# Attention of the first block: stationary values, moving turned probabilities, two heads on the two column halves of TensorE, output turned

## The chip, the cores and the metric

The kernel runs on one core of a Trainium2 chip. The metric is the device time of one execution in microseconds (us). Before the change three runs gave 3089.05, 3087.79 and 3084.29 us, median 3087.79 us.

## The reference

The program is two two-layer transformer blocks, one behind the other, on 256 tokens of width 1024, all in fp32. The first block works on two streams, X (the tokens) and Z (256 context tokens). Its token mixing has four branches of 256 columns each: a Fourier mix, neighborhood attention (`na`), a gated linear attention (`gla`) and grouped attention (`gqa`). The two attentions are what the change touches:

```python
s = jnp.einsum('bqhgd,bkhd->bhgqk', q_blk, k).astype(jnp.float32)
p = jax.nn.softmax(s, axis=-1).astype(v.dtype)
return jnp.einsum('bhgqk,bkhd->bqhgd', p, v)
...
out_x = jnp.concatenate([a_x, b_x, c_x, d_x], axis=-1)
...
x = x + mx[5] * (mix_x @ w_out[l])
```

Heads are 64 wide. Four heads and two blocks of 128 queries make 8 units per attention. The mixed result (256 x 1024) is then multiplied by `w_out`. In layer 0 both streams are mixed, in layer 1 only X.

## The kernel before

The work is an ordered list of weight pieces of 1 MB. SP loads each into a ring of four buffers (`wr`). ACT writes the high part of a piece to `wh` (L267), DVE the rest to `wl` (L278), each in two halves, and PE multiplies three times (L120, L121, L122: high by high, low by high, high by low). ACT splits piece m+2 and DVE piece m+1 while PE has piece m. Pieces of the modulation are used whole: PE multiplies them in four column tiles of 32 (L777), and DVE turns or adds the sums (L809, L817, L802).

The small work (norms, attention, turning) is cut into steps and woven in between. Every engine runs through the same pieces and in each piece through the same number of steps (`Piece.steps`, 4, or 1 or 2 for modulation), so a step with a given number lies in the same piece on every engine, but not at the same place in it: PE spreads its steps over a piece's matmuls, DVE does the first half of the next `wl` ahead of its first step, the second half ahead of its second, and a projection's `gated` (L905) or `gated_lo` (L856) ahead of its last two. Each engine's queue is in order.

Attention takes the units in pairs (two heads), 8 pairs per stream and layer: Z in layer 0 with 256 keys, X in layer 0 and X in layer 1 with 512. For a pair: PE's scores (`score`, L1948), DVE's row maximum (`peak`, L1992, or L1989 with the bias of `na`), ACT's exponential with its row sum (`exp`, L1973), PE's transposes of the probabilities (`turn`, L1955), ACT's copy of them to SBUF (`move`, L1979), PE's product with the values (`weigh`, L1963), and DVE's reciprocal of the sums (`invert`, L1997) and scaling of the output into `mix` (`keep`, L2002). In layer 0 (`PairAttention`) a pair takes 6 steps of each engine: score and peak 0 in step 0, peak 1 in step 1, exp 0 and 1 in steps 1 and 2, turn in step 3, move and invert in step 4, weigh and keep in step 5. In layer 1 (`WideAttention`) pairs overlap, a step holding score i, weigh i-2 and turn i-1, beside modulation pieces of one step each. Every fp32 matmul is two records in the trace, a transpose one.

`weigh` has the turned probabilities as the stationary operand (128 columns) and the values as the moving one (64 columns): 2 heads x 4 key blocks x 2 records = 16 for a pair with 512 keys, 8 with 256. `MixTurn` then transposes all of `mix` (16 transposes in two PSUM banks, L2122), ACT and DVE split it into `xt_hi` and `xt_lo` (L2135, L2143), and the projection by `w_out` (`ResidualOut`, four pieces) follows.

Of the kernel before, what the change touches and what calls it, by code (L numbers as in the profile page):

```python
# [196 lines left out]
class Woven:  # L197
# [36 lines left out]
    def queue(self, pieces):  # L234

        for p in pieces:
            p.m, p.u0, p.parted_before = len(self.pieces), self.units, sum(q.parted for q in self.pieces)
            self.units += p.n_units
            self.pieces.append(p)

    def load(self, sp, m):

        if m >= len(self.pieces):
            self.follow.load(sp, m - len(self.pieces))
            return
        if m >= RING:
            sp.wait_ge(self.used.sem, m - RING + 1 + self.pieces[m].held_back)
        src = self.pieces[m].src
        a, b = src.shape[1], src.shape[2]
        dst = self.raw[m % RING][:, 0:a * b].rearrange("p (a b) -> p a b", b=b)  # L250
        sp.dma_start(dst, src).then_inc(self.loaded[m % RING].sem, 16)

# [4 lines left out]
    def hi(self, act, m, h, own=False):  # L257

        if m >= len(self.pieces):
            self.follow.hi(act, m - len(self.pieces), h)  # L260
            return
        if not self.pieces[m].parted or (self.pieces[m] in self.own_hi and not own):
            return
        s, r = m % RING, self.half(m, h)
        if h == 0:
            act.wait_ge(self.loaded[s].sem, self.loaded[s].at(m // RING + 1))
        act.activation(self.high[s][:, r], self.raw[s][:, r], ACT.Copy).then_inc(self.highs.sem, 1)  # L267
# [34 lines left out]
    def whole(self, pe, m):  # L302

        s = m % RING
        pe.wait_ge(self.loaded[s].sem, self.loaded[s].at(m // RING + 1))
        return self.raw[s][:, :].rearrange("p (k n) -> p k n", n=D)
# [38 lines left out]
class Piece:  # L345
# [3 lines left out]

    n_units, steps, fetch, parted, cover, held_back = 1, 4, (), True, 0, 0  # L350

# [3 lines left out]
    def after(self, *stages):  # L355
        self.requires += stages
        return self

    def sp(self, sp):
# [1552 lines left out]
class PairAttention(Stage):  # L1912


    def __init__(self, w, pairs, buf, before, mask=None):
# [13 lines left out]
    def wait_done(self, eng):  # L1929
        eng.wait_ge(self.done.sem, self.done.at(2 * self.n))  # L1930

# [61 lines left out]

    def invert(self, dve, i):
        buf, both = self.buf, slice(2 * (i % 2), 2 * (i % 2) + 2)
        dve.wait_ge(self.probs.sem, self.probs.at(2 * i + 2))
        self.w.dve_link(dve.reciprocal(buf["inv"][:, both, 0:1], buf["sums"][:, both, 0:1]))  # L1997

    def keep(self, dve, i, bank):
        for t in range(2):  # L2000
            dve.wait_ge(self.sums.sem, self.sums.at(2 * i + t + 1))
            dve.tensor_scalar(self.pairs[i][t]["out"], self.w.ps[:, bank + t, 0:HD], self.buf["inv"][:, 2 * (i % 2) + t, 0:1], None,  # L2002
                              ALU.mult).then_inc(self.done.sem, 1)

    def pe(self, pe):
        w = self.w
        self.before(pe)
        for i in range(self.n):
# [6 lines left out]
            self.weigh(pe, i, 4)  # L2015
            for t in range(2):
                w.hold(4 + t, lambda pe_, c=2 * i + t + 1: pe_.wait_ge(self.done.sem, self.done.at(c)))
            yield
# [24 lines left out]


class WideAttention(PairAttention):
# [9 lines left out]
    def pe(self, pe):  # L2055
# [5 lines left out]
        for i in range(n + 2):  # L2061
# [6 lines left out]
            if i >= 2:  # L2068
                if i >= 3:
                    pe.wait_ge(self.done.sem, self.done.at(2 * (i - 2)))  # L2070
                self.weigh(pe, i - 2, 4)
            if 1 <= i <= n:
# [25 lines left out]


class MixTurn(Stage):  # L2100

    n_steps = 4

    def __init__(self, w, mix, pair, need, room):
        super().__init__(w)
        self.mix, self.pair, self.need, self.room = mix, pair, need, room
        self.turned, self.highs, self.moved = w.share("mix_turned", 4), w.share("mix_high", 4), w.share("mix_low", 4)

# [3 lines left out]
    def pe(self, pe):  # L2114
        w = self.w
        for b in range(4):
            self.need(pe, b)
            w.open(pe, 4 + b % 2)
            for i in range(2):
                for t in range(2):  # L2120
                    k = 2 * b + i
                    last = pe.transpose(w.ps[:, 4 + b % 2, i * 256 + t * P:i * 256 + (t + 1) * P], self.mix[:, t, k * P:(k + 1) * P], w.eye)  # L2122
            last.then_inc(self.turned.sem, 1)
            w.hold(4 + b % 2, lambda pe_, n=b + 1: pe_.wait_ge(self.moved.sem, self.moved.at(n)))
            yield

    def view(self, b):
        return self.w.ps[:, 4 + b % 2, :].rearrange("p (k n) -> p k n", k=2)

    def act(self, act):  # L2130
        for b in range(4):
            if b == 0:
                self.room(act)
            act.wait_ge(self.turned.sem, self.turned.at(b + 1))
            act.activation(self.pair[0][:, 2 * b:2 * b + 2, :], self.view(b), ACT.Copy).then_inc(self.highs.sem, 1)  # L2135
            yield

    def dve(self, dve):
        for b in range(4):
            if b == 0:  # L2140
                self.room(dve)
            dve.wait_ge(self.highs.sem, self.highs.at(b + 1))
            dve.tensor_tensor(self.pair[1][:, 2 * b:2 * b + 2, :], self.view(b), self.pair[0][:, 2 * b:2 * b + 2, :].bitcast(F32),  # L2143
                              ALU.subtract).then_inc(self.moved.sem, 1)
            yield

class SecondWoven:
# [4 lines left out]
    def __init__(self, c, base, first):  # L2152
# [13 lines left out]
        self.parts = 0  # L2166
        self.dve_step, self.act_step, self.pool_step = (self.share(f"{e}_link", 0) for e in ("dve", "act", "pool"))

# [1052 lines left out]
def second_block(c, A, x, eye, angles, out, base, first):  # L3221
# [325 lines left out]
    def scalar(act):  # L3547
        w.act_link = Chain(act, w.act_step)
        for s in segments:
            s.run("act", act)  # L3550

    def vector(dve):
        w.dve_link = Chain(dve, w.dve_step)
        for s in segments:
            s.run("dve", dve)

    def gpsimd(pool):
        w.pool_link = Chain(pool, w.pool_step)
        for p_ in pools:
# [143 lines left out]
def first_block(w, A, c):  # L3703
# [102 lines left out]
    class Mixers:  # L3806
# [96 lines left out]
        def attention(self, *ready):  # L3903
            s, z = self.s, self.s is Z

            def near(hh, qt):
                r, n = slice(64 * (hh % 2), 64 * (hh % 2) + 64), slice(64 * hh, 64 * hh + 64)
                keys, vs = zna_k[r, hh // 2, :] if z else self.na_keys[r, hh // 2, :], [zna_v[:, j, n] for j in range(2)]
                u = dict(q=self.na_t[r, hh // 2, qt * P:(qt + 1) * P], keys=keys, v=vs, out=mix[:, qt, 256 + 64 * hh:320 + 64 * hh])
                if not z:  # L3910
# [4 lines left out]
            def grouped(hh, qt):  # L3915
                kv = hh // 2
                n = slice(HD * kv, HD * kv + HD)
                u = dict(q=self.g_t[n, hh % 2, qt * P:(qt + 1) * P], keys=zg_k[n, :] if z else self.gqa_keys[n, :], v=[zg_v[:, j, n] for j in range(2)],
                         out=mix[:, qt, 768 + HD * hh:768 + HD * hh + HD])
                if not z:  # L3920
# [18 lines left out]
            self.turn = MixTurn(w, mix, s.pair, waits(self.na.wait_done, self.gqa.wait_done, self.gla_norm.wait_done, self.fourier.wait_done),  # L3939
                                lambda eng: None)  # L3940
            return both + [self.turn]
# [298 lines left out]
```

## Time and profile before

| what | value |
|---|---|
| median of three runs | 3087.79 us (3084.29 to 3089.05) |
| the profiled execution, its own time | 3091.58 us |
| its span | 3089.8 us |
| mean granted TensorE clock | 0.991 |
| PE, matmul | 2984.7 us busy, 97% |
| PEld, weight load | 2736.9 us, 89% |
| DVE | 1754.1 us, 57% |
| ACT | 1461.9 us, 47% |
| attention of Z, layer 0 | about 430 to 513 us |
| attention of X, layer 0 | about 780 to 890 us |
| attention of X, layer 1 | 1746 to 1793 us |

How to read it: a matmul's duration is longer than the distance to the next one, since matmuls are pipelined, so the cost of a run of matmuls is read from the starts. The profiled execution is 3.8 us above the median of the three runs. The page's line of the chain that ended last is 85% PE.

### The profile page before, as it was taken

The numbers are of one execution on the slowest core, as the hardware profiler recorded it, in microseconds if no ns is written. First come the engines' busy times: TensorE is split into PE (matmuls) and PEld (weight loads), VectorE is DVE, ScalarE is ACT, GpSimd is POOL, SyncE is SP. The second block draws the span as 40 slices with busy tenths as digits, with TensorE's granted clock in tenths as the row PEclk, the third lists the DMA queues.
The fourth block names the chain that finished last, engine by engine and source line by source line (L and its number), as shares of the span: only waits on it lengthen the run. The fifth ranks groups of instructions, "written<-read, shape, count | busy, mean of one in ns | idle before, by whom it ended". The sixth has DMA issues, their size and how long they took to land.

```text
span 3089.8 us, 53353 instructions
## 1 busy us (share of the span) xinstructions
PE 2984.7 (97%) x22944; PEld 2736.9 (89%) x22944; DVE 1754.1 (57%) x2618; ACT 1461.9 (47%) x2162; POOL 152.3 (5%) x148
## 2 busy tenths in 40 slices
PE   8999999999999999999999999999999999999998
PEld 6899888898789998899898889999999989999997
DVE  4446555656447545455655455564766656475655
ACT  4335445453545443444444444455654445565443
POOL 0000000001000000000200000001110101110000
PEclk9999999999999999999999999999999999999999
DMA  7875446664465566765365446554455655445563
GB/s 281 282 237 171 153 156 201 223 197 147 154 202 173 185 199 204 263 226 172 117 197 177 159 156 191 198 172 129 121 175 185 197 190 161 127 130 160 177 197 131
DMA packets 411990, 561.95 MB, mean 182 GB/s; under 512 B 26300, under 2 KB 359020, under 8 KB 411372
## 3 DMA queue, kind: packets, MB, share of 16 engines
q1 hardware_dynamic: 411756, 558.55, 55.7%
q8 instruction: 182, 2.98, 0.4%
q14 instruction: 52, 0.43, 0.0%
HBM read 557.41 MB, written 1.10 MB: 181 GB/s over the span
## 4 chain that ended last, share of the span: by engine, by line
PE 85%; DVE 7%; ACT 3%; DMA 2%; issue 2%; SPq 0%; POOL 0%; DVEq 0%; ACTq 0%
PE psum L120 24%; PE psum L122 24%; PE psum L121 24%; DMA wr<-in_ffn_w_dram 2%; PE psum L777 1%; DVE wl L278 1%; PE psum L2471 1%; PE psum L1238 1%; PE psum L1963 1%; PE psum L2387 1%; PE psum L2462 1%; DVE wl L2221 1%; PE psum L1586 1%; PE psum L128 1%; PE psum L1573 1%
## 5 line engine op out<-in xcount | busy, mean ns | idle before, releaser
L278 DVE TENSOR_TENSOR wl<-wr,wh 128x1024 fp32r<-128x1024 f32 (+1 forms) x558 | 658.8, 1215 | 238.1 <-ACT wh L267 236.6
L267 ACT ACTIVATE wh<-wr 128x1024 fp32r<-128x1024 f32 (+1 forms) x558 | 554.9, 1039 | 247.2 <-DMA wr<-in_ffn_w_dram 224.8
L120 PE MATMUL psum<-xt_hi,wh 128*128 128x256 f32 (+1 forms) x2000 | 565.6, 283 | 4.3 <-DVE wl L278 3.2
L122 PE MATMUL psum<-xt_hi,wl 128*128 128x256 f32 (+1 forms) x2000 | 558.0, 279 | 0.0
L121 PE MATMUL psum<-xt_lo,wh 128*128 128x256 f32 (+1 forms) x2000 | 558.0, 279 | 0.0
L2221 DVE TENSOR_TENSOR wl<-wr,wh 128x1024 fp32r<-128x1024 f32 (+3 forms) x336 | 390.9, 1199 | 124.2 <-ACT wh L2213 123.4
L120 PEld LDWEIGHTS psum<-xt_hi,wh 128*128 128x128 f32 (+1 forms) x2000 | 377.4, 189 | 15.8 <-issue 8.6
L121 PEld LDWEIGHTS psum<-xt_lo,wh 128*128 128x128 f32 (+1 forms) x2000 | 376.9, 188 | 2.3
L122 PEld LDWEIGHTS psum<-xt_hi,wl 128*128 128x128 f32 (+1 forms) x2000 | 377.8, 189 | 0.1
L2213 ACT ACTIVATE wh<-wr 128x1024 fp32r<-128x1024 f32 (+3 forms) x336 | 323.4, 999 | 106.3 <-DMA wr<-in_mlp_w_dram 76.4
L120 PE MATMUL psum<-wh,xt_hi 128*128 128x256 f32 (+1 forms) x1280 | 364.8, 285 | 2.4 <-ACT vv L3378 1.8
L121 PE MATMUL psum<-wl,xt_hi 128*128 128x256 f32 (+1 forms) x1280 | 356.3, 278 | 0.0
L122 PE MATMUL psum<-wh,xt_lo 128*128 128x256 f32 (+1 forms) x1280 | 356.2, 278 | 0.0
L120 PE MATMUL psum<-zt_hi,wh 128*128 128x256 f32 (+1 forms) x1072 | 309.2, 288 | 4.8 <-DVE wl L278 4.1
L121 PE MATMUL psum<-zt_lo,wh 128*128 128x256 f32 (+1 forms) x1072 | 299.6, 279 | 0.0
L122 PE MATMUL psum<-zt_hi,wl 128*128 128x256 f32 (+1 forms) x1072 | 299.4, 279 | 0.0
L120 PE MATMUL psum<-wh,gated_hi 128*128 128x512 f32 x616 | 251.1, 408 | 3.9 <-DVE wl L278 2.7
L120 PEld LDWEIGHTS psum<-wh,xt_hi 128*128 128x128 f32 x1280 | 241.5, 189 | 3.5 <-DVE wl L2221 2.4
L122 PE MATMUL psum<-wh,gated_lo 128*128 128x512 f32 x616 | 243.9, 396 | 0.0
L121 PE MATMUL psum<-wl,gated_hi 128*128 128x512 f32 x616 | 243.5, 395 | 0.0
L122 PEld LDWEIGHTS psum<-wh,xt_lo 128*128 128x128 f32 x1280 | 241.5, 189 | 0.0
L121 PEld LDWEIGHTS psum<-wl,xt_hi 128*128 128x128 f32 x1280 | 241.0, 188 | 0.1
(462 smaller groups left out, 5254.0 us busy)
## 6 DMA issues: line engine op xcount, KB each, us to landing
wr<-in_ffn_w_dram SPq DMA_DIRECT2D x231, 1024.0 KB, 5.4
wr<-in_w_in_dram SPq DMA_DIRECT2D x88, 1024.0 KB, 5.3
wr<-in_w_mod_dram SPq DMA_DIRECT2D x72, 1024.0 KB, 5.1
wr<-in_mlp_w_dram SPq DMA_DIRECT2D x64, 1024.0 KB, 5.4
wr<-in_w_out_dram SPq DMA_DIRECT2D x20, 1024.0 KB, 5.3
wr<-in_mem_w_kv_dram SPq DMA_DIRECT2D x8, 1024.0 KB, 5.1
wr<-in_w_branch_dram SPq DMA_DIRECT2D x16, 512.0 KB, 3.5
wr<-in_w_branch_dram SPq DMA_DIRECT2D x8, 1024.0 KB, 5.2
```

The source lines that it names most:

```text
L120: pe.matmul(out, a[0], b[0], start=first, stop=False)
L121: pe.matmul(out, a[0], b[1], start=False, stop=False)
L122: return pe.matmul(out, a[1], b[0], start=False, stop=last)
L128: pe.matmul(out, eye, eye, start=True, stop=True)
L267: act.activation(self.high[s][:, r], self.raw[s][:, r], ACT.Copy).then_inc(self.highs.sem, 1)
L278: dve.tensor_tensor(self.low[s][:, r], self.raw[s][:, r], self.high[s][:, r].bitcast(F32), ALU.subtract).then_inc(self.lows.sem, 1)
L777: last = pe.matmul(self.group_rows(j), b["silu"][:, at:at + MOD_COLS], cols[:, j], start=(k == 0), stop=(k == 1), tile_position=(0, j * MO ...
L1238: return pe.matmul(out, self.x[:, t, k * P:(k + 1) * P], self.b["diag"][:, t, :], start=True, stop=True)
L1573: last = pe.matmul(w.ps[:, 4, at:at + P], a[:, t, d * P:(d + 1) * P], dec[:, tab, :], start=True, stop=True)
L1586: last = pe.matmul(w.ps[:, 4 + i, pair * 256 + t * P:pair * 256 + (t + 1) * P], src[:, 256 + jt * P:256 + (jt + 1) * P], src[:, it * P:(it ...
L2213: act.activation(self.high[s][:, r], self.raw[s][:, r], ACT.Copy).then_inc(self.highs.sem, 1)
L2221: dve.tensor_tensor(self.low[s][:, r], self.raw[s][:, r], self.high[s][:, r].bitcast(F32), ALU.subtract).then_inc(self.lows.sem, 1)
```

## The change

- `weigh` makes the values the stationary operand (64 columns) and the turned probabilities the moving one (128 columns). The two heads of a pair go to columns 0 to 63 and 64 to 127 of the array and to the two halves of the partitions of one PSUM bank, alternating by key block. The number of matmuls stays. The result is the output turned: features on partitions, queries along the row.
- The row sums now lie along the wrong axis, so the probabilities are scaled before they are turned: `scale` (a reciprocal of one column, then a multiplication of 128 x 256 or 128 x 512 in place) for each head, and `turn` waits for it in place of `exp`. In layer 0 it stands in DVE's steps 2 and 3, in layer 1 ahead of the peaks of the next pair. `invert` is gone, and `keep` is one copy of 128 x 128 in place of two scalings of 128 x 64.
- In layer 1 weigh alternates between banks 4 and 5.
- `mix` holds the two attentions turned, so `MixTurn` transposes only the Fourier and gla parts (8 transposes), and ACT and DVE split the rest from SBUF. Its order is Fourier, gla, na, gqa, each with a wait of its own.
- `OutPiece` loads a piece of the first block's `w_out` with three transfers in place of one, since the rows that belong to gqa come in another order.
- The second block goes on with the link semaphores of the first.

```diff
 class OutPiece(ProjectionPiece):
+    n_loads = 3
...
+        out = [(dst[:, 0:6, :], self.src[:, 0:6, :])]
+        for a in range(2):
+            rows = w2d[6 * P + a * P:6 * P + (a + 1) * P, c0:c0 + cw].rearrange("(b d) n -> d b n", d=HD)
+            out.append((dst[a * HD:(a + 1) * HD, 6:8, :], rows))
...
     def turn(self, pe, i, bank):
         for t in range(2):
-            pe.wait_ge(self.probs.sem, self.probs.at(2 * i + t + 1))
+            pe.wait_ge(self.scaled.sem, self.scaled.at(2 * i + t + 1))
...
     def weigh(self, pe, i, bank):
         m = self.width(i) // P
-        for t in range(2):
-            pe.wait_ge(self.moved.sem, self.moved.at(2 * i + t + 1))
-            for j in range(m):
-                last = pe.matmul(self.w.ps[:, bank + t, 0:HD], self.buf["pt"][:, t, j * P:(j + 1) * P], self.pairs[i][t]["v"][j],
-                                 start=(j == 0), stop=(j == m - 1))
-            last.then_inc(self.sums.sem, 1)
+        pe.wait_ge(self.moved.sem, self.moved.at(2 * i + 2))
+        for j in range(m):
+            for t in range(2):
+                last = pe.matmul(self.w.ps[t * HD:(t + 1) * HD, bank, 0:P], self.pairs[i][t]["v"][j], self.buf["pt"][:, t, j * P:(j + 1) * P],
+                                 start=(j == 0), stop=(j == m - 1), tile_position=(0, t * HD))
+        last.then_inc(self.sums.sem, 1)
...
-    def invert(self, dve, i):
...
+    def scale(self, dve, i, t):
+        buf, n = self.buf, 2 * (i % 2) + t
+        dve.wait_ge(self.probs.sem, self.probs.at(2 * i + t + 1))
+        self.w.dve_link(dve.reciprocal(buf["inv"][:, n, 0:1], buf["sums"][:, n, 0:1]))
+        p = self.probs_of(i, t)[:, 0:self.width(i)]
+        dve.tensor_scalar(p, p, buf["inv"][:, n, 0:1], None, ALU.mult).then_inc(self.scaled.sem, 1)
 
     def keep(self, dve, i, bank):
...
+        dve.wait_ge(self.sums.sem, self.sums.at(i + 1))
+        dve.tensor_copy(self.pairs[i][0]["out"], self.w.ps[:, bank, 0:P]).then_inc(self.done.sem, 1)
...
             self.peak(dve, i, 1, 4)
-            yield from [None] * 3
-            self.invert(dve, i)
             yield
+            self.scale(dve, i, 0)
+            yield
+            self.scale(dve, i, 1)
+            yield from [None] * 2
             self.keep(dve, i, 4)
             yield
...
+            if 1 <= i <= self.n:
+                self.scale(dve, i - 1, 0)
+                self.scale(dve, i - 1, 1)
             if i < self.n:
                 self.peak(dve, i, 0, 0)
                 self.peak(dve, i, 1, 0)
             if i >= 2:
-                self.keep(dve, i - 2, 4)
-            if 1 <= i <= self.n:
-                self.invert(dve, i - 1)
+                self.keep(dve, i - 2, 4 + i % 2)
```

On DVE, pair 1 of Z in layer 0 (counted from 0), at 444 to 451 us of the trace before: L1992 is peak 0 and peak 1, L278 the two halves of a `wl`. Before:

```order
L1992 TENSOR_REDUCE head_neg<-psum 128x1
L809 STREAM_TRANSPOSE mod_turned<-psum 128x256
L817 SCALAR_TENSOR_TENSOR mod<-mod_turned,mod 128x16
L278 TENSOR_TENSOR wl_53<-wr_49,wh_57 128x1024
L1992 TENSOR_REDUCE head_neg<-psum 128x1
L278 TENSOR_TENSOR wl_53<-wr_49,wh_57 128x1024
L856 TENSOR_TENSOR gated_lo<-gated,gated_hi 128x512
L1997 RECIPROCAL head_inv<-head_sums 128x2
L2002 TENSOR_SCALAR mix<-psum,head_inv 128x64 x2
```

The same place in the changed program:

```order
L814 STREAM_TRANSPOSE mod_turned<-psum 128x256
L822 SCALAR_TENSOR_TENSOR mod<-mod_turned,mod 128x16
L280 TENSOR_TENSOR wl_53<-wr_49,wh_57 128x1024
L2013 TENSOR_REDUCE head_neg<-psum 128x1
L280 TENSOR_TENSOR wl_53<-wr_49,wh_57 128x1024
L2018 RECIPROCAL head_inv<-head_sums 128x1
L2020 TENSOR_SCALAR probs_130<-probs_130,head_inv 128x256
L861 TENSOR_TENSOR gated_lo<-gated,gated_hi 128x512
L2018 RECIPROCAL head_inv<-head_sums 128x1
L2020 TENSOR_SCALAR probs_130<-probs_130,head_inv 128x256
L2024 COPY mix<-psum 128x128
```

The first scale (L2018, L2020) stands behind both halves of `wl`, the second also behind `gated_lo`, and PE's transposes of this pair wait for them.

On DVE, one step of X's attention in layer 1, at 1762.7 to 1766.1 us of the trace before. Before:

```order
L809 STREAM_TRANSPOSE mod_turned<-psum 128x256
L817 SCALAR_TENSOR_TENSOR mod<-mod_turned,mod 128x16
L1992 TENSOR_REDUCE head_neg<-psum 128x1 x2
L2002 TENSOR_SCALAR mix<-psum,head_inv 128x64 x2
L1997 RECIPROCAL head_inv<-head_sums 128x2
```

The same step in the changed program:

```order
L814 STREAM_TRANSPOSE mod_turned<-psum 128x256
L822 SCALAR_TENSOR_TENSOR mod<-mod_turned,mod 128x16
L2018 RECIPROCAL head_inv<-head_sums 128x1
L2020 TENSOR_SCALAR probs_180<-probs_180,head_inv 128x512
L2018 RECIPROCAL head_inv<-head_sums 128x1
L2020 TENSOR_SCALAR probs_180<-probs_180,head_inv 128x512
L2013 TENSOR_REDUCE head_neg<-psum 128x1 x2
L2024 COPY mix<-psum 128x128
```

The two scales of the pair before stand ahead of this pair's peaks.

## Rows read from the trace of the kernel before

**Rows 1.** The page, busy time and share of the span of each engine
```profile
PE 2984.7 (97%) x22944; PEld 2736.9 (89%) x22944; DVE 1754.1 (57%) x2618; ACT 1461.9 (47%) x2162; POOL 152.3 (5%) x148
```

**Rows 2.** Waits of PE in 430:900: total us, times, longest
```profile
PE psum L1955 <- ACT probs L1973: 6.5, 5, 2.5
PE psum L120 <- DVE wl L278: 3.8, 3, 1.9
```

**Rows 3.** Timeline of one step in layer 1, PE and PEld: start, us
```profile
1757.68 1.13 PE L1948 MATMUL psum<-na_keys,na_t 64*128 64x512 f32 x4
1758.73 0.52 PEld L1963 LDWEIGHTS psum<-hx,probs_t 128*128 128x128 f32 x4 [0.76 <-issue]
1759.17 0.53 PEld L1963 LDWEIGHTS psum<-z_na_v,probs_t 128*128 128x128 f32 x4
...
1760.46 0.92 PEld L1955 LDWEIGHTS psum<-eye,probs 128*128 128x128 f32 x8
1761.54 1.07 PE L777 MATMUL psum<-wr,silu_cond 128*32 128x256 f32 x16
1761.54 0.59 PEld L777 LDWEIGHTS psum<-wr,silu_cond 128*32 128x32 f32 x16 [0.17 <-issue]
1762.54 0.30 PEld L128 LDWEIGHTS psum<-eye 128*128 128x128 f32 x2 [0.41 <-issue]
```

**Rows 4.** Groups on DVE that price the scale: us busy, mean ns of one
```profile
L1266 DVE TENSOR_SCALAR diag<-eye,row_small 128x128 f32<-128x128 f32 x22 | 5.3, 283 | 0.4
L1997 DVE RECIPROCAL head_inv<-head_sums 128x2 f32<-128x2 f32 x24 | 3.8, 158 | 2.4 <-ACT probs L1973 2.4
L2961 DVE TENSOR_SCALAR x<-x,ln_mv,ln_rstd 128x1024 f32<-128x1024 f32 x3 | 2.4, 809 | 0.0
```

**Rows 5.** Timeline, Z in layer 0: pair 1, then pair 3
```profile
446.43 1.22 DVE L278 TENSOR_TENSOR wl<-wr,wh 128x1024 fp32r<-128x1024 f32 x1
447.16 0.20 PEld L1955 LDWEIGHTS psum<-eye,probs 128*128 128x128 f32 x2 [0.15 <-ACT probs L1973]
447.66 0.69 DVE L856 TENSOR_TENSOR gated_lo<-gated,gated_hi 128x512 fp32r<-128x512 f32 x1
...
466.36 0.60 PE L1955 MATMUL psum<-eye,probs 128*128 128x128 f32 x4
466.56 0.69 DVE L905 TENSOR_TENSOR gated<-silu,psum 128x512 f32<-128x512 f32 x1 [3.39 <-PE psum L122]
```

**Rows 6.** Timeline, X in layer 0, pair 6
```profile
871.16 1.23 DVE L278 TENSOR_TENSOR wl<-wr,wh 128x1024 fp32r<-128x1024 f32 x1 [0.80 <-ACT wh L267]
871.89 0.66 PE L1955 MATMUL psum<-eye,probs 128*128 128x128 f32 x4 [1.00 <-ACT probs L1973]
```

**Rows 7.** Timeline in layer 1: the step of rows 3, then the one with wl
```profile
1757.93 0.17 DVE L817 SCALAR_TENSOR_TENSOR mod<-mod_turned,mod 128x16 f32<-128x16 f32 x1
1758.85 0.69 DVE L1989 CUSTOM_DVE_ANT_1 masked<-psum,na_table 128x512 f32<-128x512 f32 x1 [0.74 <-PE psum L1948]
...
1773.54 1.13 PE L1948 MATMUL psum<-gqa_keys,gqa_t 64*128 64x512 f32 x4
1773.85 2.36 DVE L278 TENSOR_TENSOR wl<-wr,wh 128x1024 fp32r<-128x1024 f32 x2
1776.13 1.28 DVE L1992 TENSOR_REDUCE head_neg<-psum 128x1 f32<-128x512 f32 x2
```

**Rows 8.** Timeline of PE at the end of layer 1's attention, first and last
```profile
1786.32 0.63 PE L1963 MATMUL psum<-hx,probs_t 128*128 128x64 f32 x4
...
1793.58 0.36 PE L120 MATMUL psum<-wh,xt_hi 128*128 128x256 f32 x1 [0.57 <-issue]
```

**Rows 9.** A wait of PE, and windows: busy, then PEclk, DMA share
```profile
789.54 1.11 PE L1955 MATMUL psum<-eye,probs 128*128 128x128 f32 x4 [2.47 <-ACT probs L1973]
...
786.00:797.00 11.00, 8.03 (x46) 7.43 (x44) 2.87 (x5) 5.82 (x9) 0.00 (x0) 0.69 0.40 161
430.00:520.00 90.00, 87.43 (x662) 74.62 (x661) 44.99 (x81) 48.78 (x90) 0.00 (x0) 0.98 0.54 182
```

**Rows 10.** The page's DMA issues, us to landing
```profile
wr<-in_w_out_dram SPq DMA_DIRECT2D x20, 1024.0 KB, 5.3
```

More of the change, by code:

```diff
@@ L250, in load @@
         dst = self.raw[m % RING][:, 0:a * b].rearrange("p (a b) -> p a b", b=b)
-        sp.dma_start(dst, src).then_inc(self.loaded[m % RING].sem, 16)
+        for to, rows in self.pieces[m].transfers(dst):
+            sp.dma_start(to, rows).then_inc(self.loaded[m % RING].sem, 16)
     def half(self, m, h):
@@ L265, in hi @@
         if h == 0:
-            act.wait_ge(self.loaded[s].sem, self.loaded[s].at(m // RING + 1))
+            act.wait_ge(self.loaded[s].sem, self.loaded[s].at(self.pieces[m].landed))
         act.activation(self.high[s][:, r], self.raw[s][:, r], ACT.Copy).then_inc(self.highs.sem, 1)
@@ L304, in whole @@
         s = m % RING
-        pe.wait_ge(self.loaded[s].sem, self.loaded[s].at(m // RING + 1))
+        pe.wait_ge(self.loaded[s].sem, self.loaded[s].at(self.pieces[m].landed))
         return self.raw[s][:, :].rearrange("p (k n) -> p k n", n=D)
@@ L345 @@
 class Piece:
-    n_units, steps, fetch, parted, cover, held_back = 1, 4, (), True, 0, 0
+    n_units, steps, fetch, parted, cover, held_back, n_loads = 1, 4, (), True, 0, 0, 1
     def __init__(self, w, src):
@@ L357, in after, with transfers @@
         return self
+    def transfers(self, dst):
+        return [(dst, self.src)]
     def sp(self, sp):
@@ L2015, in pe @@
             self.weigh(pe, i, 4)
-            for t in range(2):
-                w.hold(4 + t, lambda pe_, c=2 * i + t + 1: pe_.wait_ge(self.done.sem, self.done.at(c)))
+            w.hold(4, lambda pe_, c=i + 1: pe_.wait_ge(self.done.sem, self.done.at(c)))
             yield
@@ L2068, in pe @@
             if i >= 2:
-                if i >= 3:
-                    pe.wait_ge(self.done.sem, self.done.at(2 * (i - 2)))
-                self.weigh(pe, i - 2, 4)
+                if i >= 4:
+                    pe.wait_ge(self.done.sem, self.done.at(i - 3))
+                self.weigh(pe, i - 2, 4 + i % 2)
             if 1 <= i <= n:
@@ L2104, with __init__ @@
     n_steps = 4
-    def __init__(self, w, mix, pair, need, room):
+    order = (0, 2, 1, 3)
+    def __init__(self, w, mix, pair, need, bank):
         super().__init__(w)
-        self.mix, self.pair, self.need, self.room = mix, pair, need, room
-        self.turned, self.highs, self.moved = w.share("mix_turned", 4), w.share("mix_high", 4), w.share("mix_low", 4)
+        self.mix, self.pair, self.need, self.bank = mix, pair, need, bank
+        self.turned, self.highs, self.moved = w.share("mix_turned", 2), w.share("mix_high", 4), w.share("mix_low", 4)
     def wait_done(self, eng):
@@ L2115, in pe @@
         w = self.w
[L2116 to L2124, printed above, removed]
+        for n, b in enumerate(self.order):
+            if n < 2:
+                self.need[b](pe)
+                bank = self.bank + n
+                if bank >= 4:
+                    w.open(pe, bank)
+                for i in range(2):
+                    for t in range(2):
+                        k = 2 * b + i
+                        last = pe.transpose(w.ps[:, bank, i * 256 + t * P:i * 256 + (t + 1) * P], self.mix[:, t, k * P:(k + 1) * P], w.eye)
+                last.then_inc(self.turned.sem, 1)
+                if bank >= 4:
+                    w.hold(bank, lambda pe_, n=n + 1: pe_.wait_ge(self.moved.sem, self.moved.at(n)))
@@ L2125, in pe, with view @@
             yield
-    def view(self, b):
-        return self.w.ps[:, 4 + b % 2, :].rearrange("p (k n) -> p k n", k=2)
+    def view(self, n, b):
+        if n < 2:
+            return self.w.ps[:, self.bank + n, :].rearrange("p (k n) -> p k n", k=2)
+        return self.mix[:, :, 2 * b * P:(2 * b + 2) * P]
     def act(self, act):
[L2131 to L2135, printed above, removed]
+        for n, b in enumerate(self.order):
+            if n < 2:
+                act.wait_ge(self.turned.sem, self.turned.at(n + 1))
+            else:
+                self.need[b](act)
+            act.activation(self.pair[0][:, 2 * b:2 * b + 2, :], self.view(n, b), ACT.Copy).then_inc(self.highs.sem, 1)
@@ L2136, in act @@
             yield
     def dve(self, dve):
[L2139 to L2143, printed above, removed]
+        for n, b in enumerate(self.order):
+            dve.wait_ge(self.highs.sem, self.highs.at(n + 1))
+            dve.tensor_tensor(self.pair[1][:, 2 * b:2 * b + 2, :], self.view(n, b), self.pair[0][:, 2 * b:2 * b + 2, :].bitcast(F32),
@@ L3547, in scalar @@
     def scalar(act):
-        w.act_link = Chain(act, w.act_step)
+        w.act_link = first["w"].act_link
         for s in segments:
@@ L3552, in vector @@
     def vector(dve):
-        w.dve_link = Chain(dve, w.dve_step)
+        w.dve_link = first["w"].dve_link
         for s in segments:
@@ L3557, in gpsimd @@
     def gpsimd(pool):
[L3558 removed]
+        w.pool_link = first["w"].pool_link
         for p_ in pools:
@@ L3938, in attention @@
                 both = [self.gqa, self.bias_turn, self.na]
-            self.turn = MixTurn(w, mix, s.pair, waits(self.na.wait_done, self.gqa.wait_done, self.gla_norm.wait_done, self.fourier.wait_done),
-                                lambda eng: None)
+            own_free = (lambda eng: self.na.emptied(eng, self.na.n - 1)) if self.wide else self.na.wait_done
+            self.turn = MixTurn(w, mix, s.pair, {0: waits(self.fourier.wait_done, own_free), 2: self.gla_norm.wait_done,
+                                                 1: self.na.wait_done, 3: self.gqa.wait_done}, 0 if self.wide else 4)
             return both + [self.turn]
```

24 lines of the change are left out of this document (12 added, 12 removed).

## The prediction

> **What bounds the kernel now.** I read the page first: PE's matmuls cover 97% of the span, DVE 57% and ACT 47% [rows 1]. So whatever shortens PE's own work shortens the kernel, and whatever makes PE wait adds to it, with nothing to absorb it. DVE's share says nothing about when a DVE result is there. The waits of PE come next: between 430 and 900 us, where both attentions of layer 0 lie, it waited 6.5 us in five places for exponentials and 3.8 us for `wl` [rows 2]. That is nearly all; PE is otherwise fed. Last come the timelines of single pairs, which show what a transposition costs, what stands on DVE when PE wants the probabilities, and how much time is between.
>
> **The product with the values.** Four records take 0.44 us (1758.73 to 1759.17), 0.11 each, so 16 take 1.76 us and 8 take 0.88 [rows 3]. How fast would two column halves go? The trace has column tiles: L777, 16 records of 256 columns each, in 1.07 us with the tail of the last. Eight transposes of 128 columns take 0.92 us, 0.11 each, so 256 columns take 0.21, and 16 one after another would be 3.4 us. Four tiles therefore run at once [rows 3]. I take the same for two halves: 8 groups of 0.11 us, 0.87 in all, and 0.43 for 256 keys. That saves 0.89 us for a pair with 512 keys and 0.45 for one with 256. The far bound is no overlap at all, which saves nothing.
>
> Against this stands the change of tiling. Behind L777 the weight load idled 0.41 us; 0.21 of it is the last group's streaming, so 0.2 is lost. Ahead of L777 it idled 0.17, of which I charge 0.15 [rows 3]. In layer 0 ten pairs have ordinary matmuls on both sides of `weigh` (0.35 each), five have them on one side (0.17), one has tiled work on both sides: 4.4 us. Gross, the 8 pairs of Z save 3.6 and the 8 of X 7.1; **net 6.3 us saved in layer 0**. The Trainium skill, page TensorEngine Tiling (Array Packing), section Key Properties, has the rule: changing the tiling mode drains the engine. The trace agrees (the 0.41 us). If a change of mode cost nothing, the sum below would be lower by the 4.4 us, about zero.
>
> **The transposes of mix.** Each mixed stream has 8 fewer. At 0.11 us the 16 that go in layer 0 save **1.8 us**. Layer 1's belong to its end, below.
>
> **What scaling costs on DVE.** A reciprocal is 0.16 us. The multiplication is not in the trace; 128 x 128 from SBUF took 0.28 us and 128 x 1024 took 0.81 [rows 4]. On the line between them 256 columns take 0.36 and 512 take 0.51, and I keep 0.28 and 0.81 as ends. With two hand-overs of 0.04 a scale is 0.6 us for 256 keys and 0.75 for 512. The copy of 128 x 128 replaces two scalings; it runs after PE's work and is hidden. DVE has the room: 24 pairs x about 1.2 us in 3090. The question is only where each scale stands.
>
> **The wait it adds.** `turn` is PE's step 3 and the second scale DVE's step 3. PE's step can lie at the start of a piece, while DVE's has one or two halves of `wl`, `gated` or `gated_lo` ahead. Before, PE waited for `exp` alone, a step earlier. Behind the transposes PE's queue holds the main matmuls, so the wait stops everything, and ACT's move of the probabilities with it. For each pair I took from the timeline when PE began the second head's transposes and when the instruction ahead of the second scale ended:
> - Z pair 1: PE at 447.16; `wl` until 447.65, then scale 0 (0.6), `gated_lo` (0.69), scale 1 (0.6): 449.5, 2.4 us late [rows 5]. Z pair 6 has the same pattern: together 4.8.
> - Z pair 3: PE began at 466.36, the second head 0.2 later; `gated` ends at 467.25, scale 1 at 467.9: 1.4 late [rows 5]. With X pairs 3 and 5 (1.55, 0.65): 3.6.
> - X pair 6: PE at 871.89; `wl` ends at 872.39, scale 1 at 873.15: 1.25 late [rows 6]. Of this kind are seven, the others Z 2, 4, 7 (0.6, 1.4, 0.6) and X 0, 1, 4 (1.3, 0.1, 1.15): 6.4.
> - The other four pairs have their scales early enough: nothing.
>
> Sum **14.8 us added**. DVE is held there by work that PE itself released (the previous piece's end), so a wait of PE does not bring DVE ahead for the next pair, and I count all of it. With the ends 0.28 and 0.81 for the multiplication it would be 12 to 20.
>
> **Layer 1.** A step is 5.3 us of gapless PE, 1757.68 to 1762.96. It has tiled work ahead of `weigh` already, so only the exit is new: 0.89 - 0.2 = 0.69 saved, in five steps 3.4 us. DVE is free from 1758.10, the scales end at 1759.6; the new turn falls 2.1 us behind the scores' start, at 1759.8, so they fit by 0.2 [rows 3, 7]. The peaks move from 1758.85 to 1759.6, which the next scores can bear. The first turn waits 0.5. In the step at 1773.54 two halves of `wl` stand ahead, until 1776.21 [rows 7]; they come later still, since ACT's moves and its `wh` follow later exponentials, I estimate by 1.4 us. The scales then end 5.6 us behind the scores, and the step takes some 7.8 in place of 5.3: 2.5 lost (at best nothing). At the end, from the last `weigh` at 1786.32 to the projection at 1793.58 there are 7.3 us [rows 8], a chain of transposes, splits, and again; with `weigh` 0.9 shorter, eight transposes and no second round over the same banks I count 5.2, 2.1 saved, less 0.2 because `weigh` now waits for both moves. Layer 1: -3.4 + 0.5 + 2.5 - 2.1 + 0.2 = **2.3 us saved**.
>
> **Transfers.** Twelve pieces of `w_out` come in three transfers, same bytes, landing 5.3 us after issue [rows 10], more than a piece ahead of ACT's need; SP has room. Nothing; if it were 1 us later each, still nothing until `wl` is late.
>
> **Sum.** -6.3 - 1.8 - 2.3 + 14.8 = **+4.4 us**. The profiled execution took 3091.58, so 3096.0 in its terms. It stood 3.8 us above the median 3087.79, so by the median I forecast **3092.2 us**. About 0.2%, 6.2 us, is what a measurement of this kernel can tell from no change: 3081.6 to 3094.0 is the same.
>
> **The rivals.**
> 1. *The waits are mostly absorbed* (faster): where PE loses 2 us, ACT and DVE finish their splits meanwhile, and later pairs find the scale done. For it: before two of the late pairs DVE itself waited for `wh` [rows 6]. Against: in Z pair 1 DVE is busy without a gap. With a third of the waits left, 5 us, the sum is -5.4, 3082; with none, 3077. Chance 0.27.
> 2. *The clock falls* (slower): a wait of 2.47 us at 787 us was followed by a mean granted clock of 0.69 over 786 to 797 [rows 9], the lower level of 1.2 GHz for some 6.8 us, worth 3.4. Over the 90 us from 430 it was 0.98, which is 1.8 us [rows 9]. Six of the new waits are 1.3 us or more. It decides if three or more bring a fall: each costs 1.7 us or more, 5 to 10 together, giving 3097 to 3102. Chance 0.12.
> 3. *Weights of the halves are not loaded under a running matmul.* A half's load is 64 columns; two are the 0.055 us that a load of 128 cost beside each 64-column matmul of before (0.11 less the matmul's half) [rows 3]. A group would take 0.165, costing 0.43 for each of 16 pairs and 0.22 for 8: 8.6 more, 3101. Chance 0.04. The Trainium skill, page TensorE: Matmul & The Clock Gate, section Packing small matmuls, row/col tiling, says that a load overlaps a running matmul only when the row group differs, and here both halves use all rows. The trace speaks against it: L777 has all 128 rows too, and its loads were hidden [rows 3].
> 4. *The change doesn't do what it says*: no overlap of the halves. Then 3.6 + 7.1 + 4.5 (five steps of layer 1 at 0.89) are missing: 3107. Chance 0.03.
>
> The forecast itself, waits of 10 to 17 us and gains of 8 to 13, holds 0.54: 3085 to 3098.
>
> **Numbers.** Faster: most of rival 1 and a sliver of the forecast, 0.19. Slower than 3094.0: a third of the forecast and rivals 2 to 4, 0.35. The same: 0.46. The range that should hold it 8 times in 10 takes in most of rivals 1 and 2: 3079 to 3101.
>
> **What would show it.** Right: the product with the values is 16 records in under 1 us; PE waits for `probs` from the multiplication (L2020) about 15 us in layer 0, longest 2.4, in twelve places; steps of layer 1 are near 4.6 us, one near 8. Wrong: fewer than 6 us of such waits (rival 1), a granted clock below 0.985 (rival 2), groups of 0.16 us (3) or of 0.21 (4).

## The result, and the profile after

| what | before | after |
|---|---|---|
| median | 3089.3 us (9 runs) | 3097.5 us (9 runs, 3093.6 to 3101.4) |
| profiled execution | 3091.58 us | 3101.36 us |

The ratio of the runs taken side by side is 1.0023, with a 95% interval of 1.0015 to 1.0032: **8.2 us slower** by the medians, 7.1 by the ratio. The profiled execution of after is 3.9 us above its median.

The page's busy time and, by waits, what PE waited for between 420 and 910 us, where layer 0's attentions now lie (total, times, longest):

```profile
PE 2982.0 (96%) x22920; PEld 2724.1 (88%) x22920; DVE 1769.6 (57%) x2666; ACT 1461.9 (47%) x2162; POOL 151.9 (5%) x148
```
```profile
PE psum L1976 <- DVE probs L2020: 15.1, 13, 2.2
PE psum L120 <- DVE wl L280: 3.7, 2, 1.9
```

The transposes (L1976) waited 15.1 us for the multiplication. Before they had waited 6.5 us for the exponential [rows 2], so 8.6 are new. Layer 1 adds one wait of 1.94 us, shown below; over the whole execution the new waits are 10.6 us. PE's busy share fell with the new waits, DVE's did not matter.

The product with the values, the X pair of layer 0 first in order; timeline of PE before, then after (start, us):

```profile
796.60 0.28 PE L122 MATMUL psum<-zt_hi,wl 128*128 128x256 f32 x1
796.72 0.55 PE L1963 MATMUL psum<-hx,probs_t 128*128 128x64 f32 x4
...
798.42 0.36 PE L120 MATMUL psum<-zt_hi,wh 128*128 128x256 f32 x1
```
```profile
804.83 0.28 PE L122 MATMUL psum<-zt_hi,wl 128*128 128x256 f32 x1
805.04 0.66 PE L1984 MATMUL psum<-probs_t,hx 128*64 128x128 f32 x8
805.53 0.61 PE L1984 MATMUL psum<-probs_t,z_gqa_v 128*64 128x128 f32 x8
806.06 0.38 PE L120 MATMUL psum<-zt_hi,wh 128*128 128x256 f32 x1
```

From the main matmul ahead to the one behind it was 1.82 us and is 1.23, drains included. The 16 records take 1.02.

Scales on DVE, groups by form, and Z's pair 1 in the timeline:

```profile
L2020 DVE TENSOR_SCALAR probs<-probs,head_inv 128x512 f32<-128x512 f32 x32 | 15.6, 487 | 1.1
L2018 DVE RECIPROCAL head_inv<-head_sums 128x1 f32<-128x1 f32 x48 | 7.6, 158 | 4.5 <-ACT probs L1994 4.4
...
L2020 DVE TENSOR_SCALAR probs<-probs,head_inv 128x256 f32<-128x256 f32 x16 | 5.7, 354 | 0.6
```
```profile
447.01 1.22 DVE L280 TENSOR_TENSOR wl<-wr,wh 128x1024 fp32r<-128x1024 f32 x1
...
448.14 0.15 DVE L2018 RECIPROCAL head_inv<-head_sums 128x1 f32<-128x1 f32 x1
448.33 0.35 DVE L2020 TENSOR_SCALAR probs<-probs,head_inv 128x256 f32<-128x256 f32 x1
448.60 0.69 DVE L861 TENSOR_TENSOR gated_lo<-gated,gated_hi 128x512 fp32r<-128x512 f32 x1
...
448.74 0.44 PE L1976 MATMUL psum<-eye,probs 128*128 128x128 f32 x2 [1.22 <-DVE probs L2020]
...
449.80 0.44 PE L1976 MATMUL psum<-eye,probs 128*128 128x128 f32 x2 [0.62 <-DVE probs L2020]
```

This is the order of waits that the prediction drew [rows 5]; only a scale takes 0.46 us, from its reciprocal to the next instruction's start, where I had 0.6.

Layer 1, PE: the steps' scores and the end.

```profile
1760.82 1.13 PE L1969 MATMUL psum<-na_keys,na_t 64*128 64x512 f32 x4
...
1765.41 1.13 PE L1969 MATMUL psum<-na_keys,na_t 64*128 64x512 f32 x4
```
```profile
1778.98 1.13 PE L1969 MATMUL psum<-gqa_keys,gqa_t 64*128 64x512 f32 x4
...
1783.08 1.91 PE L1976 MATMUL psum<-eye,probs 128*128 128x128 f32 x8 [1.94 <-DVE probs L2020]
...
1787.14 1.13 PE L1969 MATMUL psum<-gqa_keys,gqa_t 64*128 64x512 f32 x4
...
1791.68 0.66 PE L1984 MATMUL psum<-probs_t,hx 128*64 128x128 f32 x8 [1.14 <-ACT probs_t L2000]
...
1794.63 0.66 PE L1984 MATMUL psum<-probs_t,hx 128*64 128x128 f32 x8 [0.61 <-ACT probs_t L2000]
...
1799.57 0.36 PE L120 MATMUL psum<-wh,xt_hi 128*128 128x256 f32 x1 [1.93 <-issue]
```

This step is 4.59 us, the three behind it are 4.53, and before it was 5.3 [rows 3]. The one behind `wl` is 8.16. The last two products wait for ACT's copies, 1.14 and 0.61 us.

The clock. Windows of after (PE busy is the first pair of numbers; granted clock, DMA share and GB/s stand last), and the stretches before that answer to them, to within some 3 us:

```profile
502.00:514.00 12.00, 10.24 (x62) 8.38 (x61) 4.31 (x11) 6.46 (x12) 0.00 (x0) 0.86 0.50 161
583.00:592.00 9.00, 7.26 (x24) 5.76 (x25) 4.38 (x5) 2.19 (x3) 0.00 (x0) 0.81 1.05 292
...
1780.00:1790.00 10.00, 8.06 (x71) 5.19 (x70) 7.88 (x18) 6.18 (x13) 0.00 (x0) 0.83 0.53 155
1798.00:1806.00 8.00, 6.43 (x42) 6.47 (x43) 3.73 (x5) 4.25 (x5) 0.00 (x0) 0.79 0.01 2
```
```profile
496.00:508.00 12.00, 11.99 (x82) 10.38 (x83) 7.07 (x14) 8.45 (x17) 0.00 (x0) 1.00 0.79 274
580.00:589.00 9.00, 9.00 (x60) 8.12 (x59) 6.75 (x8) 5.23 (x7) 0.00 (x0) 1.00 1.00 322
...
1771.00:1781.00 10.00, 10.00 (x89) 6.74 (x89) 6.21 (x13) 7.73 (x14) 0.00 (x0) 1.00 0.59 187
1790.00:1798.00 8.00, 6.54 (x55) 6.23 (x56) 4.84 (x6) 5.50 (x8) 0.00 (x0) 1.00 0.00 0
```

Four stretches that had been at 2.4 GHz each lost 1.7 us, (1 - 0.86) x 12, a spell of 3.4 us at 1.2 GHz. Three are behind waits of the change: those of Z's pair 6, layer 1's wait for the scale, and its end. The fourth, at 585 us, is not: it follows a wait of 1.95 us for `wl` that the kernel before has too, at 579 us, there without a spell. Such spells also come and go where the work is the same:

```profile
2569.00:2581.00 12.00, 9.87 (x58) 9.27 (x59) 10.27 (x12) 8.41 (x14) 3.61 (x2) 0.72 0.09 29
```
```profile
2560.00:2572.00 12.00, 9.27 (x80) 8.60 (x78) 9.53 (x19) 9.64 (x14) 1.19 (x1) 1.00 0.20 56
```

The first line is after, the second before; (1 - 0.72) x 12 is 3.4 us, two spells' worth. The mean granted clock of the profiled execution is 0.987, was 0.991. How much of the 8.2 us is the clock, one trace can't say; the runs below can.

### The profile page after: what moved, and what is told of

It reads as the page before. It is cut to its first block, busy times and chain, and to the rows that moved or that the text cites. A ratio compares the mean times of both kernels' runs of the same rounds, so it can differ in the third digit from the quotient of the medians.

```text
span 3099.4 us, 53326 instructions
## 1 busy us (share of the span) xinstructions
PE 2982.0 (96%) x22920; PEld 2724.1 (88%) x22920; DVE 1769.6 (57%) x2666; ACT 1461.9 (47%) x2162; POOL 151.9 (5%) x148
## 4 chain that ended last, share of the span: by engine, by line
PE 84%; DVE 8%; ACT 3%; DMA 2%; issue 2%; SPq 0%; POOL 0%; DVEq 0%; ACTq 0%
PE psum L120 24%; PE psum L122 24%; PE psum L121 24%; PE psum L782 2%; DVE wl L280 1%; DMA wr<-in_ffn_w_dram 1%; PE psum L2498 1%; PE psum L2489 1%; DVE wl L2248 1%; PE psum L2414 1%; PE psum L1606 1%; PE psum L128 1%; PE psum L1243 1%; PE psum L1593 1%; PE psum L1976 1%
## 5 line engine op out<-in xcount | busy, mean ns | idle before, releaser
L120 PEld LDWEIGHTS psum<-xt_hi,wh 128*128 128x128 f32 (+1 forms) x2000 | 377.4, 189 | 14.8 <-issue 7.5
```

The source lines that it names most:

```text
L120: pe.matmul(out, a[0], b[0], start=first, stop=False)
```

## The experiments

Each kernel was timed beside the kernel before, whose medians were 3090.1 us for E1 to E4, 3091.1 for E5 to E8 and 3090.0 for E9 to E11. Two theories are told apart: the cost is the waits' own length (the record's), or part of it is the clock that falls behind them.

**E1, the scale left out, E4, the scale alone.** The two halves of the sum.

```diff
     def turn(self, pe, i, bank):
-            pe.wait_ge(self.scaled.sem, self.scaled.at(2 * i + t + 1))
+            pe.wait_ge(self.probs.sem, self.probs.at(2 * i + t + 1))
...
-                self.scale(dve, i - 1, 0)
-                self.scale(dve, i - 1, 1)
```

E4 starts from the kernel before and gets `scale`, its places and the wait in `turn`; `keep` copies 128 x 64 twice.

> The changed kernel with the 48 scales on DVE left out, and the transposes waiting for the exponentials as before the change; the attention outputs are therefore not divided by their row sums. If the waits for the scale are what the change costs (my step), they go and the gains stay. Of the 17.1 us that the changed kernel's PE waited for the scale, the 6.5 us that the kernel before waited for exponentials come back, so 10.6 go, and with them the clock falls at 506.6, 585.1, 1783.2 and 1800.3 us of its trace (up to 6.8 us): 3080 to 3087 us, ratio to before 0.997 to 0.999, and the first half is faster than before. If the time was lost to clock falls that have nothing to do with the waits, or to the drains around the column halves, it stays at 3095 to 3098.

> The kernel before with the scaling alone: probabilities scaled ahead of the transposes, as in the change, and the outputs copied; the product with the values, the layout of mix, its 16 transposes and the single transfers stay as before. By my step this has the added waits and none of the gains: +14.8 in layer 0 and +3.0 in layer 1, 17.8 us, 3107, ratio 1.0058. By the changed kernel's trace the waits for probabilities grew by 10.6 us only (6.5 to 17.1): with up to four further clock falls that is 3100 to 3106. If the scaling costs nothing and the product or the layout is what made the kernel slower, it is 3088 to 3091.

E1: **3079.9 us**, ratio 0.9971 (0.9961 to 0.9980). E4: **3107.3 us**, 1.0062 (1.0048 to 1.0076). Waits of PE, the whole of E1, then of E4:

```profile
PE psum L1976 <- ACT probs L1994: 4.9, 5, 1.7
```
```profile
PE psum L1956 <- DVE probs L2000: 17.0, 14, 2.8
```

Scaling costs 17.2 us alone (E4 against before) and 17.6 in the change (after against E1), the other parts gain 10.2 (E1 against before), and -10.2 + 17.2 is nearly the +8.2 measured: the parts add up. But E4's waits for the scaled probabilities are 17.0 us where the kernel before had 6.5, so 10.5 of the 17.2 are waits and some 7 are something else.

**E6, the waits filled, E9, its control, E10, layer 1 alone.** `cover` puts matmuls of the identity into PE's queue, whose results nobody uses; the kernel already has it at other places.

```diff
     def turn(self, pe, i, bank):
         for t in range(2):
+            self.w.cover(pe, self.fill.get((i, t), 0))
             pe.wait_ge(self.scaled.sem, self.scaled.at(2 * i + t + 1))
```

> The changed kernel with matmuls of the identity (results unused) put in front of those waits of PE that are new with the change and 0.5 us or longer: 4, 2, 3, 8, 6, 4, 2 in Z, 4, 5, 4, 2, 3, 5 in X of layer 0, 7 in layer 1's step behind wl, 4 and 2 more in its last two steps, 7 more ahead of the projection. The waits' length stays, only PE is not idle in them. My record holds the waits' own length to be nearly all of the cost: then nothing changes, 3096 to 3100. By the comparison of the profiles since (extra half-clock spells near 507, 1783 and 1800 us, and a mean clock of 0.987 against 0.991) part of the cost is the clock: then two to four spells of 3.4 us go, each worth 1.7, and it is 3090 to 3094.

> The control to the filled kernel: the kernel before the change with matmuls of the identity in its own waits for exponentials (6 and 3 in Z's pair 4, 9 and 1 in X's pair 0, 3 in X's pair 6) and 2 more ahead of layer 1's projection. If filling gave 9 us because it took away what the change had added, it gives little here, 0 to 3.4 us (the two half-clock spells at 479 and 789 us): 3087 to 3091. If filling makes any such kernel faster by as much, 3080 to 3083.

> The changed kernel with the filling in layer 1 alone (7 matmuls in the step behind wl, 4 and 2 more in the last two steps, 7 more ahead of the projection). The spells at 1783 and 1800 us of the changed kernel's trace should go, 3.4 us: 3093 to 3095. If it is 3097 or more, those two spells were chance; if 3089, layer 0's filling did nothing.

E6: **3088.6 us**, 0.9992 (0.9983 to 1.0001). E9: 3088.0 us, 0.9996 (0.9987 to 1.0005). E10: 3095.1 us, 1.0017 (1.0008 to 1.0026). Z's pair 6 in E6, timeline of PE, and the windows of E6 that answer to those of after:

```profile
501.20 1.05 PE L128 MATMUL psum<-eye 128*128 128x128 f32 x8
...
502.50 0.44 PE L1979 MATMUL psum<-eye,probs 128*128 128x128 f32 x2 [0.24 <-DVE probs L2023]
502.78 0.61 PE L128 MATMUL psum<-eye 128*128 128x128 f32 x4
503.56 0.44 PE L1979 MATMUL psum<-eye,probs 128*128 128x128 f32 x2 [0.17 <-DVE probs L2023]
```
```profile
500.00:512.00 12.00, 11.58 (x81) 9.58 (x80) 5.78 (x14) 7.89 (x14) 0.00 (x0) 1.00 0.65 217
581.00:590.00 9.00, 8.56 (x47) 7.16 (x48) 4.53 (x6) 4.02 (x4) 0.00 (x0) 1.00 1.11 294
1771.00:1781.00 10.00, 9.81 (x94) 6.76 (x91) 7.96 (x18) 6.73 (x13) 0.00 (x0) 1.00 0.65 195
1789.00:1797.00 8.00, 7.64 (x68) 7.47 (x67) 4.40 (x7) 4.20 (x5) 0.00 (x0) 1.00 0.00 0
```

The transposes of the two heads start 1.06 us apart as before the filling: DVE sets them. Only PE's idle time is gone, and with it 8.9 us, 1.4 beyond the range that I had expected if the clock were part of the cost. The spells behind the three waits of the change are gone as well. The window at 581 us shows less: E6 has a spell at 598 us instead, behind a wait of 1.88 us for `wl`.

Filling the waits of the kernel before (E9) gives 2.0 us by the medians and 1.2 by the ratio, not told from nothing, with an interval up to 4.0. E6 fills those old waits too, so up to some 2 of its 8.9 us are not what the change brought. The granted clock of all runs says the same. The shortfall is the mean of (1 - granted clock) x span, the time that a full clock would have given back, had PE been busy throughout:

| kernel | runs | mean granted clock | shortfall |
|---|---|---|---|
| before, beside E9 to E11 | 27 | 0.9903 | 30.0 us |
| E9, before with its waits filled | 11 | 0.9911 | 27.5 us |
| E1, without the scale | 10 | 0.9899 | 31.1 us |
| after | 9 | 0.9882 | 36.5 us |
| E6, after with its waits filled | 11 | 0.9913 | 26.9 us |

Each shortfall is good to about 1 us. After stands 5.4 us above E1, and E6 9.6 us below after, near the 8.9 us that filling gave. **So the clock is shown to be 5 to 7 of the 17.6 us that scaling costs** (5.4 by the clocks, 8.9 - 2.0 by the filling), and the 10.6 us of new waits are the rest, to within 2 us. Layer 1's filling (E10) gave 2.4 us of it, near the 3.4 expected, but the intervals of E10 and after overlap.

**E2, the transposes a step later, E7, also layer 1's scales earlier, E11, both with filling.**

```diff
-            yield from [None] * 3
+            yield from [None] * 4
             self.turn(pe, i, 4)
-            yield from [None] * 2
+            yield
...
-            if 1 <= i <= self.n:
-                self.scale(dve, i - 1, 0)
-                self.scale(dve, i - 1, 1)
...
                 self.keep(dve, i - 2, 4 + i % 2)
+            if i < self.n:
+                self.scale(dve, i, 0)
+                self.scale(dve, i, 1)
```

> The changed kernel with PE's transposes of a layer-0 pair in its step 4 instead of 3; all else as it is, ACT's moves too. The scale is then there when PE comes, so by the theory of the waits PE's waits for it in layer 0 (15.1 us in the stretch of both attentions) fall to under 3 us. What may take their place: ACT moves both heads in its step 4 and PE weighs in step 5, one step (about 2.5 us) behind the transposes instead of two, and a move of both heads takes 1.1 us (512 keys), so I expect 0 to 5 us of new waits for probs_t. Sum: 3086 to 3093. If the moves are the real limit, it is 3095 to 3100.

> The changed kernel with two orders changed: in layer 0 PE turns in step 4 (that alone gave 3087.1), and in layer 1 the two scales of a pair stand at the end of the DVE step that found its peaks, ahead of the next wl halves. If the wait of 1.94 us behind wl and the half-clock spell after it are what layer 1 loses, they go: 3.6 us less, 3083 to 3085. If DVE then waits for the exponentials in every step (1.5 us, five to eight times) and wl comes late for PE, it is 3088 to 3093.

> Turn in step 4, layer 1's scales at the end of the step, and the waits that are left filled (1 to 6 matmuls at nine places of layer 0, 2, 7 and 2 more in layer 1's last steps, 7 more ahead of the projection). The two orders alone gave 3084.9, filling gave the changed kernel 9. Fewer waits are left here, so I expect 2 to 5 us more: 3080 to 3083, under both kernels. If the clock was already paid back by the shorter waits, it stays at 3084 to 3086.

E2: 3087.1 us, 0.9995 (0.9985 to 1.0005), 10.4 under after. Waits between 420 and 910 us:

```profile
PE psum L1976 <- DVE probs L2020: 7.5, 8, 1.7
...
PE psum L1969 <- DVE mix L2024: 1.6, 3, 0.6
PE psum L1984 <- ACT probs_t L2000: 1.2, 2, 0.6
```

The time is in the expected range, by another path: half of the waits for the scale stayed (7.5, not under 3), while a wait of 7.6 us less, with its clock, was worth 10. The copies of ACT were no limit. E7: 3084.9 us, 0.9982 (0.9973 to 0.9991); the wait behind `wl` is gone, and the end waits more:

```profile
1785.27 0.66 PE L1984 MATMUL psum<-probs_t,hx 128*64 128x128 f32 x8 [1.86 <-ACT probs_t L2000]
```

E11: **3083.3 us, 0.9978 (0.9969 to 0.9988)**, faster than both kernels, by 6.7 us against before. Over E7 the filling brings 1.6 us, less than the 2 to 5 expected and not told from nothing.

**E8, layer 1 alone.** Layer 0 with the old classes and the old order of `mix` and `w_out`:

```diff
-                self.na = PairAttention(w, na_pairs, self.buf, first)
+                self.na = OldPairAttention(w, na_pairs, self.buf, first)
```

> Layer 0 as before the change (values moving, outputs scaled, mix and w_out in the old order), layer 1 as changed. By my record layer 1 gains 2.3 us: 3087 to 3088, ratio 0.999. By the drift in the changed kernel's trace it is -0.5 us with two half-clock spells of 3.4 us in it (1783, 1800), -4.0 without them: 3086 to 3090. If the whole +7.4 us is layer 0's, this kernel is at or under the one before; if layer 1's spells carry it, it is 3092 or more.

3088.3 us, 0.9994 (0.9985 to 1.0003): 1.9 us (ratio) to 2.7 us (medians) less than before, where I had 2.3; the interval still reaches over 1. What made the whole slower is layer 0's.

**E3, one head after the other.**

```diff
-        for j in range(m):
-            for t in range(2):
+        for t in range(2):
+            for j in range(m):
```

> The changed kernel with the product of one head finished before the other's begins (columns 0 to 63, then 64 to 127), so that neighbouring matmuls never lie on different halves. If alternating halves are what lets two matmuls run at once, this costs what the form was to save: 0.89 us for each of the 16 pairs with 512 keys and 0.45 for each of 8 with 256, 17.8 us in all, of which the waits in layer 1 may swallow some: 3110 to 3116. If the overlap isn't tied to the order (each half runs its own chain in any case), it costs under 3 us: 3097 to 3100.

3101.1 us (5 runs), 1.0041 (1.0029 to 1.0053): 3.6 more than after, not 13 or more. Timeline of PE, the X pair shown above:

```profile
799.92 0.28 PE L122 MATMUL psum<-zt_hi,wl 128*128 128x256 f32 x1
800.13 0.65 PE L1984 MATMUL psum<-probs_t,hx 128*64 128x128 f32 x4
800.62 0.27 PE L1984 MATMUL psum<-probs_t,z_gqa_v 128*64 128x128 f32 x1
800.62 0.32 PE L1984 MATMUL psum<-probs_t,hx 128*64 128x128 f32 x1
...
801.11 0.60 PE L1984 MATMUL psum<-probs_t,z_gqa_v 128*64 128x128 f32 x4
801.64 0.38 PE L120 MATMUL psum<-zt_hi,wh 128*128 128x256 f32 x1
```

The first head's first four records run alone, then its second four and the other head's first four side by side, then the last four alone: 1.51 us for 16 records, where alternating takes 1.02 and no overlap would take 1.8. With 8 records, a pair of Z, there is no loss at all:

```profile
448.11 0.28 PE L122 MATMUL psum<-xt_hi,wl 128*128 128x256 f32 x1
448.31 0.66 PE L1984 MATMUL psum<-probs_t,z_na_v 128*64 128x128 f32 x8
448.91 0.50 PE L120 MATMUL psum<-wh,gated_hi 128*128 128x512 f32 x1
```

So the overlap belongs to the column halves and reaches over neighbouring records of the other half, four of them here. My first theory of E3, that the order alone makes it, fell; "under 3" was too little as well. The trace has 0.49 us lost in each of the 16 pairs with 512 keys, 7.8 in all, and the time shows 3.6 by the medians and 5.6 by the ratios. Where the rest went was not followed up; the 5 runs' clock shortfall is 33.5 us, 3 less than after's.

**E5, one transfer for each piece of `w_out`.**

```diff
-    n_loads = 3
+    n_loads = 1
```

> The changed kernel with each piece of w_out in one transfer, its rows in the order of memory; the projection by w_out therefore multiplies the gqa part with rows in another order. By my step the transfers cost nothing: the time stays at that of the changed kernel, 3097.5, within 2 us. One row speaks against it: a load of 1 MB issued at 776.8 us landed 9.6 us later before the change, one at 786.5 us in the changed kernel 7.6 us later, and the exponential of X's first pair waited for it. If the three transfers made that load faster, this kernel is up to 2 us slower (3098 to 3100) and the load takes 9 to 10 us again; if they cost something, it is 3092 to 3095.

3097.8 us, 1.0023 (1.0014 to 1.0032): the three transfers cost nothing and gain nothing. The load in question landed 8.7 us after issue, between the two others; it varies by itself.

## Why the prediction was right in its direction, and which steps failed

The forecast was +4.4 us, the result +8.2, inside the range. It lies just over the bound of 0.2%, in the class "slower", to which I had given 0.35, less than to "the same". By its terms:

- **The product with the values: right.** From load to load over all 16 pairs of layer 0 I find 1.5 us saved in Z and 4.7 in X, 6.2 (6.3 predicted); 0.70 to 0.76 for a step of layer 1 (0.69). Groups of 0.11 us, weights hidden: rivals 3 and 4 are out. The rule about loads and row groups from the Trainium skill, page TensorE: Matmul & The Clock Gate, section Packing small matmuls, row/col tiling, did not hold for these halves, which use all 128 rows and differ in their columns: 16 records took 1.02 us, their loads hidden. A change of tiling cost 0.2 us at entry and 0.2 at exit (0.31 us from load to load there, 0.11 among the neighbours), 0.15 and 0.2 predicted. The drain that the Trainium skill states, page TensorEngine Tiling (Array Packing), section Key Properties, is there.
- **The waits it adds, layer 0: +14.8 predicted, 8.5 measured.** This step failed twice. The reasoning on DVE's order was right, but a scale is 0.46 us for 256 keys and 0.60 for 512, not 0.6 and 0.75: The 0.04 that I took for a hand-over is there inside a scale (448.29 to 448.33 in the lines above). At its ends DVE starts an instruction some 0.1 before the one ahead has ended (448.14, where `wl` ends at 448.23; 448.60, where the multiplication ends at 448.68). And "a wait of PE does not bring DVE ahead for the next pair, and I count all of it" was wrong for the next pair:

| pair (wait ahead of both heads' transposes, us) | predicted | after minus before |
|---|---|---|
| Z 1, Z 6 | 2.4, 2.4 | 1.84, 1.75 |
| Z 3, Z 4 | 1.4, 1.4 | 1.03, 1.35 |
| X 3, X 4, X 6 | 1.55, 1.15, 1.25 | 1.08, 0.58, 1.15 |
| X 0 | 1.3 | -0.30 |
| Z 2, Z 7, X 1, X 5 | 0.6, 0.6, 0.1, 0.65 | 0 |

  The four that wait for nothing each stand behind a pair that waited; that the one is the other's cause is argued from this pattern alone. At X 0 ACT, ahead of the exponential, had waited 3.51 us for a load before and 1.58 after, which gave 2 us back. The sign "waits for `probs` about 15 us in layer 0" came true by luck: 14.8 was the part added to the 6.5 of before, and the 15.1 measured hold both.
- **The clock, rival 2, at 0.12: it happened**, beside the forecast and not in its place. I priced it right (1.7 us a spell, 5 to 10 together) and judged it unlikely; the runs put it at 5 to 7. Its sign, a granted clock below 0.985, was set too low: the profile has 0.987, the runs 0.9882. This is the term that the sum put at nothing: 14.8 + 3.0 for scaling was 17.8 against 17.6 measured, right by two errors that cancel, waits of 10.6 and a clock of about 7.
- **Layer 1: -2.3 predicted, -1.9 to -2.7 (E8).** Inside, the wait behind `wl` was 1.94 us with the step at 8.16 (7.8), the end from the last product to the projection 4.94 (5.2). The waits for both heads' copies, which the alternating product needs at its start, priced at 0.2, were 1.75 (1.14 and 0.61); the first turn, priced at 0.5, cost 0.27 (from the second scores to the third 3.77 us, was 3.50).
- **Rival 1, waits absorbed:** partly (of 14.8 us 8.5 stayed), and the clock hid it.
- Left open: E1 gains 10.2 us, 6.2 to 12.1 by its interval, and the terms say 13.4 less the 1.5 above. The 1.8 for the transposes of `mix` were not measured alone.

The closure: with measured terms and the 1.8 as predicted, -6.2 - 1.8 + 8.5 - 2.3 = -1.8 us without layer 0's clock. E6 is at -2.5 by its medians, but it fills old waits too; against E9, which is at -2.0, it is -0.5. The runs don't tell these apart.

## What to carry to other kernels

Waits that this change put on a saturated TensorE cost their length, 10.6 us, and 5 to 7 us more in granted clock; price both in the sum. Filling the waits with matmuls of no use tells the two apart, if the kernel before is filled as a control and the granted clock is averaged over all runs: spells in a single trace also come and go where the work is the same. A new instruction between a producer and TensorE wants its own step in a woven order: moving the consumer one step later (E2) gave back all that the change had lost. A product that alternates between two heads needs both heads' operands at its start.

## What the runs showed of the hardware

- Matmuls on the two column halves overlap even when four records of the same half stand between them in the queue (E3: 8 records, 4 for each half, 0.59 us in either order; 16 records 1.51 us apart, 1.02 alternating).
- New waits of PE of 0.5 to 2.2 us were followed, here and there, by spells of 3.4 us at 1.2 GHz. Filling them and the old ones with matmuls of no use removed those at 507, 1783 and 1800 us of after, raised the mean granted clock from 0.9882 to 0.9913, and took 8.9 us off the time; a like filling of the kernel before took off 2.0.
- The same wait of 1.95 us for `wl` was followed by such a spell in after (585 us) and in E9 (577 us), and not in before (579 us).
- A multiplication of 128 x 512 by a column took 0.49 us on DVE, in place from SBUF, and 128 x 256 took 0.35.
